# Final norm with tokens on partitions, begun inside the last products of FFN2 (decoder layer, one core)

## The chip, the cores and the metric

The kernel runs on one core of a Trainium2 chip. The time is the device time of one execution in microseconds (us), the median of three executions. The engines are named as the profile names them: PE is TensorE (PEld its weight loads), DVE is VectorE, ACT is ScalarE, POOL is GpSimd, SP is SyncE. SP issues nearly all loads and stores here.

## The reference, cut to what matters

One layer of a decoder works on 1088 tokens (1024 of a prompt, 64 of samples) of 1024 channels. Only its end matters here: the second feed-forward half step and the norm behind it.

```python
def rmsnorm(x, g):
    xf = x.astype(jnp.float32)
    y = xf * lax.rsqrt(jnp.mean(xf * xf, axis=-1, keepdims=True) + EPS)
    return (y * g.astype(jnp.float32)).astype(x.dtype)

def ffn_half_step(x, g, wg, wu, wd):
    h = rmsnorm(x, g)
    return x + 0.5 * ((jax.nn.silu(h @ wg) * (h @ wu)) @ wd)

yp = ffn_half_step(yp, ffn2_norm[l], ffn2_gate[l], ffn2_up[l], ffn2_down[l])
y_prompt = rmsnorm(yp, final_norm)
```

## The kernel before

**Layout.** The residual stream `x` lies in on-chip memory with channels on partitions: `[128, 8, 1088]`, 8 blocks of 128 channels (index d or k), the tokens along the free dimension. Token loops go over three chunks c of 384, 384 and 320 tokens. Every product is done as three passes of split operands (lines 623, 624, 625).

**Phases.** Each engine has its own instruction stream, written out by hand. Semaphores order the streams, and eleven numbered barriers (`barrier`, line 378) separate the phases: an engine drains, adds one to a shared semaphore and waits for the others. SP and POOL don't count in them; they run ahead and wait for single semaphores. Barrier 9 stands ahead of the `w_co` projection, barrier 10 ahead of the norm of FFN2, barrier 11 behind FFN2.

**FFN2.** `ffn` (PE line 635, ACT line 1135, DVE line 1523) is a loop of 11 groups of 256 hidden channels. A group first makes gate and up products into banks 0 to 3 (for each half f and chunk c, 48 matmuls). ACT takes the silu (line 1146) and rounds (1152), DVE multiplies (1542) and makes the low part (1530). Then come 24 down tiles, numbered (c, d), of 6 matmuls each, into banks 4 to 7 in turn. For each of them DVE adds half of the tile to `x` (line 1554, called the residual below). PE may write tile j only when residual j-4 is done (line 661). POOL splits the next weights (lines 569, 571) as SP's loads land; behind the last group's weights it has no work.

**Final phase.** After barrier 11, `norm` runs once more (PE 627, ACT 1119, DVE 1492) with channels on partitions. ACT squares 24 tiles of `x` (line 1126) through four buffers. PE adds them over partitions by matmuls with a matrix of ones (632), so that every partition has the token's sum. DVE scales and adds EPS (1504), ACT takes the root (1129), DVE the reciprocal of a whole 128 x 384 tile (1508) and then multiplies each of the 24 tiles of `x` by its gain and by that reciprocal, in place (1515). Only then is `x` turned: nine token tiles t of 128 tokens (the last of 64), two halves h of 512 channels, four transposes each (line 1113), into banks 0 to 3 in turn. ACT copies each half to `ytok` (1487), which has room for two token tiles, so that from t = 2 on each copy waits until the store of tile t-2 has landed (1486). SP stores each token tile, 512 KB (line 550).

```python
                act.wait_ge(F["yt"], F.base["yt"] + 2 * t + h + 1)
                if t >= 2:
                    act.wait_ge(F[f"out{t % 2}"], F.base[f"out{t % 2}"] + 16 * (t // 2))
                act.copy(ytok[0:n, t % 2, 512 * h:512 * h + 512], ps[0:n, (2 * t + h) % 4, :]).then_inc(F["tok"], 1)
```

**A phase of the same kind.** At the very start of the kernel the same statistics are taken with tokens on partitions: ACT squares a token tile and sums it along the free dimension in one instruction and the read of its accumulator (1216), DVE scales (1589), ACT takes the root of one column (1222), DVE its reciprocal (1595). The prediction takes durations from there.

Of the kernel before, what the change touches and what calls it, by code (L numbers as in the profile page):

```python
# [22 lines left out]
ALU = mybir.AluOpType  # L23
# [3 lines left out]
P = 128  # L27
D = 1024
# [14 lines left out]
EPS = 1e-6  # L43
# [56 lines left out]
def decoder_layer(nc, I, O):  # L100
# [5 lines left out]
    def alloc(stack, name, shape, dt=F32):  # L106
        return stack.enter_context(nc.sbuf_tensor(name, shape, dt))
# [15 lines left out]
    vecs = alloc(ctx, "vecs", [P, 60])  # L123
# [5 lines left out]
    early = ExitStack()  # L129
    Us = alloc(early, "Us", [P, CT, NB, PAD + TS])  # L130
    with ExitStack() as g:
        hh = alloc(g, "hh", [P, KT, T], F32R)
        hl = alloc(g, "hl", [P, KT, T], F32R)
        with ExitStack() as f:
            bh = alloc(f, "bh", [P, 2, KT, P], F32R)
            bl = alloc(f, "bl", [P, 2, KT, P], F32R)
            hidh = alloc(f, "hidh", [P, 2, T], F32R)
            hidl = alloc(f, "hidl", [P, 2, T], F32R)
            sg = alloc(f, "sg", [P, 2, 384])
            ht = alloc(f, "ht", [P, 2, 384])  # L140
            sq = alloc(f, "sq", [P, 4, 384])
            tb = alloc(f, "tb", [P, 3, 384])
            rs = alloc(f, "rs", [P, NC, 384])
        with ExitStack() as f:
# [16 lines left out]
        with ExitStack() as f:  # L161
            ytok = alloc(f, "ytok", [P, 2, D])
# [120 lines left out]
    of_tiles = {"t": NC * KT, "hi": NC * KT, "h": NC * KT}  # L283

    shared, base = {}, defaultdict(int)
    for n, adds in (("load", {"in0": 64, "in1": 64, "in2": 48, "xt": 2 * (QT + 1)}), ("n1", of_tiles | of_ffn),
                    ("nm", of_norm(NC) | of_proj(20, 12)), ("so", of_split | of_proj(8, 0)),
                    ("nx", of_norm(NC) | of_proj(8, 8)), ("sc", of_split | of_proj(8, 0)),
                    ("n2", of_norm(NC) | of_ffn), ("fin", of_norm(NC, False))):
        S[n] = Sems("g", shared, base)  # L290
        for name, v in adds.items():
            base[name] += v
    block = ctx.enter_context(nc.Block())
    x_tok = I["x_prompt"].rearrange("b t d -> (b t) d")
    xs_tok = I["x_sample"].rearrange("b t d -> (b t) d")
# [89 lines left out]
    def _(sp):  # L385
# [165 lines left out]
        sp.wait_ge(F["out0"], F.base["out0"] + 16 * ((QT + 2) // 2))  # L551
        sp.wait_ge(F["out1"], F.base["out1"] + 16 * ((QT + 1) // 2))


    @block.gpsimd
    def _(pool):
        pool.memset(ident[:], 0.0).then_inc(setup_done, 1)
        pool.memset(ones[:], 1.0).then_inc(setup_done, 1)
        pool.wait_ge(setup_done, 1)
        pool.affine_select(out=ident[:], in_=ident[:], compare_op=ALU.not_equal, fill=1.0, base=0,  # L560
                           pattern=[[-1, P]], channel_multiplier=1).then_inc(setup_done, 1)
# [55 lines left out]
    def _(pe):  # L617
        pe.sem_inc(unit_done, SLOTS)
        pe.sem_inc(row_done, 2)
        pe.wait_ge(setup_done, 3)  # L620
# [14 lines left out]
        def ffn(name, s):  # L635
            u0, c0_, r0 = UNIT[name], COL[name], ROW[name]
            with pe.Fori(0, FG) as i:
# [19 lines left out]
                for c, (c0, n) in enumerate(CHUNKS):  # L657
                    pe.wait_ge(s["hid"], s.base["hid"] + i * 6 + (NC + c + 2))
                    for d in range(KT):
                        j = c * KT + d  # L660
                        pe.wait_ge(s["res"], s.base["res"] + i * (NC * KT) + (j + 1))
                        out = ps[:, 4 + j % 4, 0:n]
                        for f in range(2):
                            mm = three(out, bh[:, f, d], bl[:, f, d], hidh[:, f, c0:c0 + n], hidl[:, f, c0:c0 + n],
                                       f == 0, f == 1)
                        if j < NC * KT - 1:
                            mm.then_inc(s["down"], 1)
                        else:
                            mm.then_inc(row_done, 2)

        def proj(name, s, nunits, chunks, ah, al, h_need):
            u0 = UNIT[name]
# [432 lines left out]
        for t in range(QT + 1):  # L1105
            n = P if t < QT else TSAMP
            pe.wait_ge(F["h"], F.base["h"] + KT * ([c for c, (c0, w) in enumerate(CHUNKS) if t * P < c0 + w][0] + 1))
            for h in range(2):
                j = 2 * t + h
                if j >= 4:  # L1110
                    pe.wait_ge(F["tok"], F.base["tok"] + j - 3)
                for k in range(4):
                    mm = pe.transpose(ps[0:n, j % 4, k * P:(k + 1) * P], x[:, 4 * h + k, t * P:t * P + n], ident[:])
                mm.then_inc(F["yt"], 1)


    @block.scalar
    def _(act):
# [15 lines left out]

        def ffn(name, s):
            c0_ = COL[name]
            with act.Fori(0, FG) as i:
                def silu(j):
                    f, c = divmod(j, NC)
                    n = CHUNKS[c][1]  # L1140
# [17 lines left out]
                hi(2 * NC - 1)  # L1158

        def store_proj(name, s, stg, nunits, first, dst):  # L1160

# [317 lines left out]
        F = S["fin"]  # L1479
        norm(F, CHUNKS, x, sq, rs, tb, hh, split=False)  # L1480
        for t in range(QT + 1):
            n = P if t < QT else TSAMP
            for h in range(2):
                act.wait_ge(F["yt"], F.base["yt"] + 2 * t + h + 1)
                if t >= 2:
                    act.wait_ge(F[f"out{t % 2}"], F.base[f"out{t % 2}"] + 16 * (t // 2))
                act.copy(ytok[0:n, t % 2, 512 * h:512 * h + 512], ps[0:n, (2 * t + h) % 4, :]).then_inc(F["tok"], 1)


    @block.vector  # L1490
    def _(dve):
# [28 lines left out]
            if split:  # L1520
                lo(KT * len(chunks) - 1)

        def ffn(name, s):
            c0_, r0_ = COL[name], ROW[name]
            with dve.Fori(0, FG) as i:
                def lo(j):
                    f, c = divmod(j, NC)
                    c0, n = CHUNKS[c]
# [18 lines left out]
                for j in range(NC * KT):  # L1547
# [4 lines left out]
                    else:  # L1552
                        dve.wait_ge(row_done, i * 2 + (2 + r0_ + 2))
                    dve.scalar_tensor_tensor(out=x[:, d, c0:c0 + n], in0=ps[:, 4 + j % 4, 0:n], scalar=0.5,  # L1554
                                             in1=x[:, d, c0:c0 + n], op0=ALU.mult, op1=ALU.add
                                             ).then_inc(s["res"], 1)

        def split_input(s):
            for c, (c0, n) in enumerate(CHUNKS):
# [74 lines left out]
        dve.tensor_copy(vecs[:], ps[:, 7, 0:60]).then_inc(L["vecs"], 1)  # L1634
# [305 lines left out]
        ffn("ffn2", S["n2"])  # L1940
        barrier(dve, 11)
        F = S["fin"]
        norm(F, CHUNKS, x, sq, rs, tb, G_FIN, hh, hl, split=False)

    ctx.close()

# [30 lines left out]
```

## Time and profile before

| | |
|---|---|
| median of 3 executions | 2907.81 us (2907.4 to 2916.08) |
| the profiled execution, own time | 2907.62 us |
| its span in the trace | 2905.8 us |
| mean granted TensorE clock | 0.963 |

Times in the trace are us from the span's start. A row of the timeline has start, length, engine, line, operation, output<-input, shapes and count; a bracket at its end tells how long the engine had been idle and what ended that. In a grouped row the numbers behind the bar are busy time and mean ns of one instruction, then the idle time ahead of them. A timeline row that merges two instructions ("x2") gives the length from the first's start to the second's end; instructions overlap, so the distance of two starts is less than the length of one.

### The profile page before, as it was taken

How to read it: one execution, taken by the hardware profiler on the slowest of the kernel's cores; microseconds unless marked ns; L12 is line 12 of the kernel's file. 1: busy time of each engine (PE TensorE's matmuls, PEld its weight loads, DVE VectorE, ACT ScalarE, POOL GpSimd, SP SyncE). 2: the span in 40 equal slices, each digit the busy share in tenths (PEclk: the TensorE clock that was granted, in tenths of full speed). 3: DMA queues.
4: the chain of work that ended last, by engine and by line, in shares of the span. 5: the costliest groups of instructions: out<-in, count | busy, mean ns of one | idle time of the engine just before them, and what ended most of it. 6: DMA issues, size and time to landing. Idle time of an engine off the chain costs nothing.

```text
span 2905.8 us, 44519 instructions
## 1 busy us (share of the span) xinstructions
PE 2666.4 (92%) x16895; PEld 2492.6 (86%) x16895; DVE 1124.5 (39%) x2110; ACT 533.8 (18%) x1178; POOL 702.9 (24%) x395
## 2 busy tenths in 40 slices
PE   6899999999998999488997988869899999999998
PEld 6899999999997999366556888739799999999997
DVE  5322222222226799633332131631523222222224
ACT  4200000000003111255221122320300000000003
POOL 4522222222220332022000210102222222222210
PEclk8999999999999999789998999989999999999999
DMA  5411111111110121144983111651111111111101
GB/s 171 145 44 43 43 43 43 43 43 43 43 43 15 44 74 63 53 154 127 287 242 108 43 46 74 229 216 44 44 44 43 43 43 43 43 43 43 43 14 62
DMA packets 214570, 223.71 MB, mean 77 GB/s; under 512 B 11466, under 2 KB 181510, under 8 KB 210403
## 3 DMA queue, kind: packets, MB, share of 16 engines
q1 hardware_dynamic: 197495, 194.54, 21.9%
q10 hardware_dynamic: 17004, 28.21, 2.6%
q8 instruction: 46, 0.75, 0.1%
q14 instruction: 25, 0.20, 0.0%
HBM read 190.05 MB, written 32.67 MB: 77 GB/s over the span
## 4 chain that ended last, share of the span: by engine, by line
PE 74%; issue 9%; DVE 7%; DMA 4%; ACT 2%; PEld 1%; DVEq 1%; SPq 1%; POOL 0%; ACTq 0%; PEldq 0%; POOLq 0%
PE ps L623 21%; PE ps L625 21%; PE ps L624 21%; DVE ya L1692 1%; PE ps L966 1%; PE ps L632 1%; PE ps L922 1%; DVE hidl L1530 1%; PE ps L849 1%; PE ps L860 1%; DMA Kw<-in_cache_win_k 1%; PE ps L936 1%; DVE hl L1497 1%; DVE rs L1508 1%; PE ps L832 1%
## 5 line engine op out<-in xcount | busy, mean ns | idle before, releaser
L623 PE MATMUL ps<-hh,wh 128*128 128x384 f32 (+1 forms) x3168 | 1039.9, 328 | 55.1 <-DVE hl L1562 29.2
L625 PE MATMUL ps<-hl,wh 128*128 128x384 f32 (+1 forms) x3168 | 1038.6, 328 | 0.0
L624 PE MATMUL ps<-hh,wl 128*128 128x384 f32 (+1 forms) x3168 | 1038.1, 328 | 0.0
L623 PEld LDWEIGHTS ps<-hh,wh 128*128 128x128 f32 x3168 | 599.5, 189 | 58.6 <-issue 57.6
L624 PEld LDWEIGHTS ps<-hh,wl 128*128 128x128 f32 x3168 | 599.6, 189 | 0.0
L625 PEld LDWEIGHTS ps<-hl,wh 128*128 128x128 f32 x3168 | 599.0, 189 | 0.0
L569 POOL CAST wh<-raw 128x1024 fp32r<-128x1024 f32 x140 | 150.9, 1078 | 1473.7 <-PE ps L625 1346.0
L1542 DVE TENSOR_TENSOR ht<-ps,sg 128x384 f32<-128x384 f32 x132 | 70.7, 536 | 927.5 <-PE ps L625 926.2
L571 POOL TENSOR_TENSOR wl<-raw,wh 128x1024 fp32r<-128x1024 f32 x148 | 378.0, 2554 | 41.7 <-ACT wh L1241 30.5
L623 PE MATMUL ps<-hidh,bh 128*128 128x384 f32 (+1 forms) x1056 | 346.5, 328 | 11.7 <-DVE x L1554 11.7
L1554 DVE SCALAR_TENSOR_TENSOR x<-ps,x 128x384 f32<-128x384 f32 (+1 forms) x528 | 276.6, 533 | 185.6 <-PE ps L625 185.1
L625 PE MATMUL ps<-hidl,bh 128*128 128x384 f32 (+1 forms) x1056 | 344.4, 326 | 0.0
L624 PE MATMUL ps<-hidh,bl 128*128 128x384 f32 (+1 forms) x1056 | 344.3, 326 | 0.0
L623 PEld LDWEIGHTS ps<-hidh,bh 128*128 128x128 f32 x1056 | 198.2, 188 | 18.4 <-DVE x L1554 18.4
L1146 ACT ACTIVATE sg<-ps 128x384 f32<-128x384 f32 x132 | 62.6, 475 | 746.5 <-PE ps L625 746.3
L624 PEld LDWEIGHTS ps<-hidh,bl 128*128 128x128 f32 x1056 | 198.2, 188 | 0.0
L625 PEld LDWEIGHTS ps<-hidl,bh 128*128 128x128 f32 x1056 | 198.2, 188 | 0.0
L1692 DVE SCALAR_TENSOR_TENSOR ya<-U,taps,ya x120 | 156.2, 1302 | 0.0
L569 POOL CAST bh<-raw 128x1024 fp32r<-128x1024 f32 x44 | 45.7, 1038 | 418.7 <-PE ps L625 417.2
L1530 DVE TENSOR_TENSOR hidl<-ht,hidh 128x384 fp32r<-128x384 f32 x132 | 133.8, 1026 | 0.1
L1146 ACT ACT_TABLE_LOAD x22 | 28.2, 1283 | 559.0 <-PE ps L625 559.0
L571 POOL TENSOR_TENSOR bl<-raw,bh 128x1024 fp32r<-128x1024 f32 x44 | 105.6, 2400 | 3.5
(215 smaller groups left out, 2168.2 us busy)
## 6 DMA issues: line engine op xcount, KB each, us to landing
raw<-in_ffn_gate SPq DMA_DIRECT2D x44, 512.0 KB, 3.8
raw<-in_ffn_up SPq DMA_DIRECT2D x44, 512.0 KB, 3.8
raw<-in_ffn_down SPq DMA_DIRECT2D x44, 512.0 KB, 3.3
Kw<-in_cache_win_k SPq DMA_DIRECT2D x48, 256.0 KB, 7.2
Vw<-in_cache_win_v SPq DMA_DIRECT2D x48, 256.0 KB
raw<-in_w_in SPq DMA_DIRECT2D x20, 512.0 KB, 3.8
Kw<-in_cache_win_k SPq DMA_DIRECT2D x8, 1024.0 KB, 11.9
Vw<-in_cache_win_v SPq DMA_DIRECT2D x8, 1024.0 KB
```

What stands on the lines that cost most here:

```text
L569: pool.tensor_copy(hi, raw[:, parity]).then_inc(w_hi, 1)
L571: pool.tensor_tensor(lo, raw[:, parity], hi.bitcast(F32), ALU.subtract).then_inc(w_split, 1)
L623: pe.matmul(out, w_hi_, a_hi, start=first, stop=False)
L624: pe.matmul(out, w_lo_, a_hi, start=False, stop=False)
L625: return pe.matmul(out, w_hi_, a_lo, start=False, stop=last)
L632: pe.matmul(ps[:, 5 + c, 0:n], ones[:], sqt[:, k % 4, 0:n], start=(k == 0), stop=(k == KT - 1)).then_inc(s["summed"], 1)
L832: mm = pe.matmul(ps[:, 2 * h + n % 2, far(t):far(t) + near(t)], qs[64 * h:64 * h + 64, p, t * P:(t + 1) * P], kTp[64 * h:64 * h + 64, p, ( ...
L1146: act.activation(sg[:, j % 2, 0:n], ps[:, 2 * (j % 2), 0:n], ACT.Silu).then_inc(s["sg"], 1)
L1530: dve.tensor_tensor(hidl[:, f, c0:c0 + n], ht[:, j % 2, 0:n], hidh[:, f, c0:c0 + n].bitcast(F32), ALU.subtract).then_inc(s["hid"], 1)
L1542: dve.tensor_tensor(ht[:, j % 2, 0:n], ps[:, 2 * (j % 2) + 1, 0:n], sg[:, j % 2, 0:n], ALU.mult).then_inc(s["prod"], 1)
L1554: dve.scalar_tensor_tensor(out=x[:, d, c0:c0 + n], in0=ps[:, 4 + j % 4, 0:n], scalar=0.5, in1=x[:, d, c0:c0 + n], op0=ALU.mult, op1=ALU.ad ...
L1692: dve.scalar_tensor_tensor(out=dst, in0=src, scalar=w, in1=dst, op0=ALU.mult, op1=ALU.add).then_inc(C["tap"], 1)
```

## The change

All parts of it stand at the end of the kernel, but for one load and a column of constants.

- The norm behind FFN2 and barrier 11 are gone. The raw `x` is turned to PSUM by PE (`turn_out`, eight transposes for a token tile, into a pair of banks that `y_bank` gives). ACT squares and sums each half out of PSUM (`y_squares`), DVE adds the two sums (`y_variance`), ACT takes the root with scale 1/1024 and EPS as its bias (`y_root`), DVE takes the reciprocal and multiplies each half by it and by the gain, from PSUM into `ytok` (`y_out`).
- `ytok` has a home for each of the nine token tiles, over the place of `hh`. No write to it waits for a store.
- The gain row is loaded broadcast to all partitions (`gain`, 512 KB written) by SP, behind the three loads of `mixx` after barrier 9. DVE waits for it ahead of FFN2.
- The loop of FFN2 runs ten times on PE, ACT and DVE, and the eleventh group is written out (on ACT for FFN1 too). In it PE turns token tile 0 behind down tile (1,3), tile 1 behind (1,7) and tile 2 behind (2,5). DVE does `y_variance` of tiles 0 and 1 behind the residuals (2,1) and (2,4), and `y_out` of them behind (2,2) and (2,5).

```diff
+        sp.dma_start(gain[:], I["final_norm"].unsqueeze(0).to_broadcast([P, D])
+                     ).then_inc(S["fin"]["small"], 16)
         col_loads("w_co", SLOTS)
         ffn_loads("ffn2")
...
-            sp.dma_start(dst, ytok[0:n, t % 2, :]).then_inc(F[f"out{t % 2}"], 16)
+            sp.dma_start(dst, ytok[0:n, t, :]).then_inc(F["out0"], 16)
...
+    def y_bank(t):
+        return (0, 2, 0, 2, 0, 2, 4, 6, 0)[t]
...
-        ffn("ffn2", S["n2"])
-        barrier(pe, 11)
-        F = S["fin"]
-        norm(F, CHUNKS, sq)
...
+        def turn_out(t):
+            n, c = P if t < QT else TSAMP, min(t // 3, NC - 1)
+            pe.wait_ge(N2["res"], N2.base["res"] + NC * KT * (FG - 1) + 4 + KT * (c + 1))
+            if t in (2, 3, 4, 5, 8):
+                pe.wait_ge(F["tok"], F.base["tok"] + 2 * ((t if t < 6 else 6) - 1))
             for h in range(2):
                 for k in range(4):
+                    mm = pe.transpose(ps[0:n, y_bank(t) + h, k * P:(k + 1) * P], x[:, 4 * h + k, t * P:t * P + n],
+                                      ident[:])
                 mm.then_inc(F["yt"], 1)
+        def beside_down(c, d):
+            for t in {(1, 3): [0], (1, 7): [1], (2, 5): [2]}.get((c, d), []):
+                turn_out(t)
+        ffn("ffn2", N2, beside_down)
+        for t in range(3, QT + 1):
+            turn_out(t)
...
-        barrier(act, 11)
-        norm(F, CHUNKS, x, sq, rs, tb, hh, split=False)
+        def y_squares(t):
+            n = P if t < QT else TSAMP
             for h in range(2):
+                j = 2 * t + h
+                act.wait_ge(F["yt"], F.base["yt"] + j + 1)
+                if t >= 4:
+                    act.wait_ge(Y["ssq"], Y.base["ssq"] + j - 7)
+                act.activation(ysq[0:n, t % 4, h, :], ps[0:n, y_bank(t) + h, :], ACT.Square,
+                               accum_out=ystat[0:n, h, t:t + 1]).then_inc(Y["ssq"], 1)
+        def y_root(t):
+            n = P if t < QT else TSAMP
+            act.wait_ge(Y["var"], Y.base["var"] + t + 1)
+            act.activation(ystat[0:n, 3, t:t + 1], ystat[0:n, 2, t:t + 1], ACT.Sqrt, bias=eps[0:n], scale=1.0 / D
+                           ).then_inc(Y["std"], 1)
+        for t in range(QT + 1):
+            y_squares(t)
+            y_root(t)
...
-        norm(F, CHUNKS, x, sq, rs, tb, G_FIN, hh, hl, split=False)
+        def y_variance(t):
+            n = P if t < QT else TSAMP
+            dve.wait_ge(Y["ssq"], Y.base["ssq"] + 2 * t + 2)
+            dve.tensor_tensor(ystat[0:n, 2, t:t + 1], ystat[0:n, 0, t:t + 1], ystat[0:n, 1, t:t + 1], ALU.add
+                              ).then_inc(Y["var"], 1)
+        def y_out(t):
+            n = P if t < QT else TSAMP
+            dve.wait_ge(Y["std"], Y.base["std"] + t + 1)
+            dve.reciprocal(ystat[0:n, 4, t:t + 1], ystat[0:n, 3, t:t + 1]).then_inc(Y["inv"], 1)
+            dve.wait_ge(Y["inv"], Y.base["inv"] + t + 1)
+            for h in range(2):
+                dve.scalar_tensor_tensor(out=ytok[0:n, t, 512 * h:512 * h + 512], in0=ps[0:n, y_bank(t) + h, :],
+                                         scalar=ystat[0:n, 4, t:t + 1], in1=gain[0:n, 512 * h:512 * h + 512],
+                                         op0=ALU.mult, op1=ALU.mult).then_inc(F["tok"], 1)
+        def beside_residual(c, d):
+            for t in {(2, 1): [0], (2, 4): [1]}.get((c, d), []):
+                y_variance(t)
+            for t in {(2, 2): [0], (2, 5): [1]}.get((c, d), []):
+                y_out(t)
+        dve.wait_ge(F["small"], F.base["small"] + 16)
+        ffn("ffn2", S["n2"], beside_residual)
+        for t in range(2, QT + 1):
+            y_variance(t)
+            y_out(t)
```

## Rows read from the trace of the kernel before

**Rows 1.** The chain that ended last, in order of time, from FFN2's last residual (start, length, what)

```profile
2865.73 0.05 DVE x L1554
...
2890.64 3.69 PE ps L1113 x16
...
2894.97 2.61 DMA out_y_prompt<-ytok
```

**Rows 2.** Instructions by line and shape, from 2866 us to the end

```profile
L1515 DVE SCALAR_TENSOR_TENSOR x<-x,vecs,rs 128x384 f32<-128x384 f32 x16 | 8.8, 607 | 0.1
L1487 ACT COPY ytok<-ps 128x512 f32<-128x512 f32 x16 | 8.7, 588 | 6.3 <-DMA out_y_prompt<-ytok 3.8 <-PE ps L1113 2.5
```

**Rows 3.** Timeline of the last down tiles and the end, DVE, ACT and SP

```profile
2854.54 0.56 DVE L1554 SCALAR_TENSOR_TENSOR x<-ps,x 128x384 f32<-128x384 f32 x1 [0.48 <-PE ps L625]
...
2858.70 0.56 DVE L1554 SCALAR_TENSOR_TENSOR x<-ps,x 128x384 f32<-128x384 f32 x1 [0.48 <-PE ps L625]
2859.57 0.49 DVE L1554 SCALAR_TENSOR_TENSOR x<-ps,x 128x320 f32<-128x320 f32 x1 [0.32 <-PE ps L625]
...
2865.73 0.49 DVE L1554 SCALAR_TENSOR_TENSOR x<-ps,x 128x320 f32<-128x320 f32 x1 [0.39 <-PE ps L625]
...
2901.44 1.06 ACT L1487 COPY ytok<-ps 64x512 f32<-64x512 f32 x2 [0.62 <-DMA out_y_prompt<-ytok]
2902.52 0.55 SPq L550 DMA_DIRECT2D out_y_sample<-ytok  x1
```

**Rows 4.** Timeline, transposes of `x` (PE) and one pair of ACT's copies

```profile
2885.86 2.03 ACT L1487 COPY ytok<-ps 128x512 f32<-128x512 f32 x4
2886.57 1.07 PE L1113 MATMUL ps<-ident,x 128*128 128x128 f32 x8 [2.31 <-DVE x L1515]
```

**Rows 5.** Timeline of the kernel's first 73 us: tokens on partitions, ACT and DVE

```profile
4.99 0.19 ACT L1216 ACTIVATION_READ_ACCUMULATOR kvtok<-xin 128x1 f32 x1
...
33.66 1.13 DVE L1621 SCALAR_TENSOR_TENSOR tb<-x,vecs,ps 128x384 f32<-128x384 f32 x2
...
66.05 0.15 DVE L1595 RECIPROCAL tstat<-tstat 128x1 f32<-128x1 f32 x1
66.24 0.29 DVE L1650 TENSOR_SCALAR diag<-ident,tstat 128x128 f32<-128x128 f32 x1
...
71.89 0.14 DVE L1589 TENSOR_SCALAR tstat<-tstat 64x1 f32<-64x1 f32 x1 [2.38 <-ACT kvtok L1216]
72.06 0.20 ACT L1222 ACTIVATE tstat<-tstat 64x1 f32<-64x1 f32 x1 [0.21 <-DVE tstat L1589]
```

**Rows 6.** All of ACT's table loads at line 1222, and DVE's copies from PSUM, whole span

```profile
L1222 ACT ACT_TABLE_LOAD  x1: 1283/1283/1283, 6.5 to 6.5; - x1
L1797 DVE COPY Kc<-ps 128x512 f32<-128x512 f32 x32 | 22.1, 691 | 47.0 <-PE ps L922 46.8
```

**Rows 7.** Stretches of time: length, busy us (count) of PE, PEld, DVE, ACT, POOL; clock, DMA share, GB/s

```profile
2886.00:2888.00 2.00, 1.07 (x8) 0.86 (x8) 2.00 (x2) 1.88 (x4) 0.00 (x0) 1.00 0.12 47
2888.00:2890.00 2.00, 0.00 (x0) 0.00 (x0) 2.00 (x5) 0.31 (x1) 0.00 (x0) 0.89 1.01 408
...
2894.00:2896.00 2.00, 2.00 (x11) 2.00 (x10) 0.29 (x1) 0.71 (x3) 0.00 (x0) 0.50 0.77 309
2896.00:2898.00 2.00, 2.00 (x17) 1.77 (x15) 0.00 (x0) 1.38 (x3) 0.00 (x0) 0.90 0.60 242
```

**Rows 8.** Around barrier 9: POOL's first split after it, and the landing of the `mixin` loads

```profile
1966.68 1.04 POOL L569 CAST wh<-raw 128x1024 fp32r<-128x1024 f32 x1 [108.98 <-PE ps L625]
...
DMA to landing us min/median/max: 6.7/10.5/13.5
```

**Rows 9.** Timeline, DVE's product (chunk 2, f=0 then f=1) in groups 0 and 10

```profile
2098.99 0.49 DVE L1542 TENSOR_TENSOR ht<-ps,sg 128x320 f32<-128x320 f32 x1 [6.03 <-PE ps L625]
...
2122.66 0.49 DVE L1542 TENSOR_TENSOR ht<-ps,sg 128x320 f32<-128x320 f32 x1 [6.01 <-PE ps L625]
...
2818.49 0.49 DVE L1542 TENSOR_TENSOR ht<-ps,sg 128x320 f32<-128x320 f32 x1 [6.01 <-PE ps L625]
...
2842.19 0.49 DVE L1542 TENSOR_TENSOR ht<-ps,sg 128x320 f32<-128x320 f32 x1 [6.01 <-PE ps L625]
```

More of the change, by code:

```diff
@@ L122, in decoder_layer @@
     ones = alloc(ctx, "ones", [P, P])
-    vecs = alloc(ctx, "vecs", [P, 60])
+    vecs = alloc(ctx, "vecs", [P, 61])
+    eps = vecs[:, 60:61]
     taps = alloc(ctx, "taps", [P, CT, CONVW])
@@ L131, in decoder_layer @@
     with ExitStack() as g:
+        with ExitStack() as f:
+            ytok = alloc(f, "ytok", [P, QT + 1, D])
+            ysq = alloc(f, "ysq", [P, 4, 2, 512])
         hh = alloc(g, "hh", [P, KT, T], F32R)
@@ L143, in decoder_layer @@
             rs = alloc(f, "rs", [P, NC, 384])
+            gain = alloc(f, "gain", [P, D])
+            ystat = alloc(f, "ystat", [P, 5, QT + 1])
         with ExitStack() as f:
@@ L160, in decoder_layer @@
             mixin = alloc(f, "mixin", [P, NC, KT, 384])
-        with ExitStack() as f:
-            ytok = alloc(f, "ytok", [P, 2, D])
         with ExitStack() as f:
@@ L285, in decoder_layer @@
     shared, base = {}, defaultdict(int)
-    for n, adds in (("load", {"in0": 64, "in1": 64, "in2": 48, "xt": 2 * (QT + 1)}), ("n1", of_tiles | of_ffn),
+    for n, adds in (("load", {"in0": 64, "in1": 64, "in2": 48, "small": 160, "xt": 2 * (QT + 1)}), ("n1", of_tiles | of_ffn),
                     ("nm", of_norm(NC) | of_proj(20, 12)), ("so", of_split | of_proj(8, 0)),
                     ("nx", of_norm(NC) | of_proj(8, 8)), ("sc", of_split | of_proj(8, 0)),
-                    ("n2", of_norm(NC) | of_ffn), ("fin", of_norm(NC, False))):
+                    ("n2", of_norm(NC) | of_ffn), ("fin", {})):
         S[n] = Sems("g", shared, base)
@@ L292, in decoder_layer @@
             base[name] += v
+    S["ys"] = Sems("st", S["st"].made, {n: MT + QT + 1 for n in ("ssq", "var", "std", "inv")})
     block = ctx.enter_context(nc.Block())
@@ L558, in _ @@
         pool.memset(ones[:], 1.0).then_inc(setup_done, 1)
+        pool.memset(eps, EPS).then_inc(setup_done, 1)
         pool.wait_ge(setup_done, 1)
@@ L619, in _ @@
         pe.sem_inc(row_done, 2)
-        pe.wait_ge(setup_done, 3)
+        pe.wait_ge(setup_done, 4)
         def three(out, w_hi_, w_lo_, a_hi, a_lo, first, last):
@@ L633, in norm, with ffn, groups @@
                               stop=(k == KT - 1)).then_inc(s["summed"], 1)
-        def ffn(name, s):
+        def ffn(name, s, beside_last=None):
             u0, c0_, r0 = UNIT[name], COL[name], ROW[name]
-            with pe.Fori(0, FG) as i:
+            def groups(i, beside=None):
                 for f in range(2):
@@ L669, in ffn @@
                             mm.then_inc(row_done, 2)
+                        if beside is not None:
+                            beside(c, d)
+            if beside_last is None:
+                with pe.Fori(0, FG) as i:
+                    groups(i)
+            else:
+                with pe.Fori(0, FG - 1) as i:
+                    groups(i)
+                groups(FG - 1, beside_last)
         def proj(name, s, nunits, chunks, ah, al, h_need):
@@ L1100, in _ @@
         norm(S["n2"], CHUNKS, sq)
-        ffn("ffn2", S["n2"])
-        barrier(pe, 11)
-        F = S["fin"]
-        norm(F, CHUNKS, sq)
-        for t in range(QT + 1):
-            n = P if t < QT else TSAMP
-            pe.wait_ge(F["h"], F.base["h"] + KT * ([c for c, (c0, w) in enumerate(CHUNKS) if t * P < c0 + w][0] + 1))
+        F, N2 = S["fin"], S["n2"]
+        def turn_out(t):
[3 more added lines that the diff above has]
+                pe.wait_ge(F["tok"], F.base["tok"] + 2 * ((t if t < 6 else 6) - 1))
             for h in range(2):
-                j = 2 * t + h
-                if j >= 4:
-                    pe.wait_ge(F["tok"], F.base["tok"] + j - 3)
                 for k in range(4):
-                    mm = pe.transpose(ps[0:n, j % 4, k * P:(k + 1) * P], x[:, 4 * h + k, t * P:t * P + n], ident[:])
+                    mm = pe.transpose(ps[0:n, y_bank(t) + h, k * P:(k + 1) * P], x[:, 4 * h + k, t * P:t * P + n],
+                                      ident[:])
                 mm.then_inc(F["yt"], 1)
+        def beside_down(c, d):
[4 more added lines that the diff above has]
+            turn_out(t)
     @block.scalar
@@ L1136, in ffn, with groups @@
             c0_ = COL[name]
-            with act.Fori(0, FG) as i:
+            def groups(i):
                 def silu(j):
@@ L1158, in ffn @@
                 hi(2 * NC - 1)
+            with act.Fori(0, FG - 1) as i:
+                groups(i)
+            groups(FG - 1)
         def store_proj(name, s, stg, nunits, first, dst):
@@ L1477, in _ @@
         ffn("ffn2", S["n2"])
-        barrier(act, 11)
-        F = S["fin"]
-        norm(F, CHUNKS, x, sq, rs, tb, hh, split=False)
-        for t in range(QT + 1):
+        F, Y = S["fin"], S["ys"]
+        def y_squares(t):
             n = P if t < QT else TSAMP
             for h in range(2):
[L1484 to L1487, printed above, removed]
+                j = 2 * t + h
[12 more added lines that the diff above has]
+            y_root(t)
     @block.vector
@@ L1521, in norm, with ffn, groups @@
                 lo(KT * len(chunks) - 1)
-        def ffn(name, s):
+        def ffn(name, s, beside_last=None):
             c0_, r0_ = COL[name], ROW[name]
-            with dve.Fori(0, FG) as i:
+            def groups(i, beside=None):
                 def lo(j):
@@ L1556, in ffn @@
                                              ).then_inc(s["res"], 1)
+                    if beside is not None:
+                        beside(c, d)
+            if beside_last is None:
+                with dve.Fori(0, FG) as i:
+                    groups(i)
+            else:
+                with dve.Fori(0, FG - 1) as i:
+                    groups(i)
+                groups(FG - 1, beside_last)
         def split_input(s):
@@ L1633, in _ @@
         dve.wait_ge(L["vecs_t"], L.base["vecs_t"] + 1)
-        dve.tensor_copy(vecs[:], ps[:, 7, 0:60]).then_inc(L["vecs"], 1)
+        dve.tensor_copy(vecs[:, 0:60], ps[:, 7, 0:60]).then_inc(L["vecs"], 1)
         dve.tensor_copy(taps[:], ps[:, 7, 64:64 + CT * CONVW].rearrange("p (k t) -> p k t", t=CONVW)
@@ L1939, in _ @@
         norm(S["n2"], CHUNKS, x, sq, rs, tb, G_FFN2, hh, hl)
-        ffn("ffn2", S["n2"])
-        barrier(dve, 11)
-        F = S["fin"]
-        norm(F, CHUNKS, x, sq, rs, tb, G_FIN, hh, hl, split=False)
+        F, Y = S["fin"], S["ys"]
+        def y_variance(t):
[22 more added lines that the diff above has]
+            y_out(t)
     ctx.close()
```

3 lines of the change are left out of this document (1 added, 2 removed).

## The prediction, before the change was run

> **What bounds the kernel now.** I read the chain of waits from its end backwards, then the instructions by line in the last 40 us, then the timeline of each engine there. The chain leaves FFN2 at 2865.73 us with the last residual; what follows is the final phase, and it takes 2905.8 - 2865.7 = 40.1 us to the end of the span [rows 1]. In it the first transpose that no longer waits for a normalised tile starts at 2890.64: some 25 us go into sums, roots, whole-tile reciprocals and the multiplications of line 1515 (16 wide ones at 0.607 us each) [rows 1, 2]. The rest goes into turning, copying and storing, where ACT waits for stores to land because `ytok` has two places: 3.8 us for full tiles [rows 2], and each such wait puts a landing of 2.61 us on the chain [rows 1]. Inside FFN2 the down tiles are PE's: DVE's residual takes 0.56 us of every 1.04, and DVE sits idle 0.48 [rows 3]. So the gain is to be found behind 2865.7, and its ceiling is 40.1 us less whatever the new end needs.
>
> **What beside the last products costs.** Three token tiles are turned inside the last group. Eight transposes take 1.07 us, 0.335 or so of it the latency of one, so they hold PE for about 0.95 us [rows 4]. PE is the bound there, so this is on the path: 3 x 0.95 = 2.85 us. ACT is idle in this stretch, its squares are covered. On DVE two `y_variance` and two `y_out` come between residuals. One `y_out` is a column reciprocal and two products of 128 x 512. Such a product is not in the trace. The nearest is the one of the same form, a column scalar and one operand in PSUM, at 384 columns: two in 1.13 us, so 0.53 from start to start and 0.60 for one [rows 5]. 64 columns more cost 0.07 us (0.49 to 0.56) [rows 3], so at 512 I take 0.67 from start to start and 0.74 for the last; from below 0.60 (the copy of 128 x 512 out of PSUM lasts 0.69) [rows 6], from above 0.9, if the two sources don't stream at that pace. With 0.19 for the reciprocal [rows 5] a `y_out` holds DVE 1.53 us. PE runs four banks ahead, 3 tiles x 0.88 us, so it does not wait.
>
> **The transition, step by step.** Product (1,3) is done at 2854.5 (its residual starts at 2854.54) and tile 0 is turned by 2855.5. Product (1,7) comes at 2859.65 instead of 2858.70, (2,0) at 2861.5 instead of 2859.57 after tile 1 is turned, (2,5) at 2865.9, the last one at 2868.6 instead of 2865.73 [rows 3]. DVE: variance 0 at 2862.8, residual (2,2), `y_out` 0 to 2865.2, two residuals, variance 1, a residual, `y_out` 1 from 2866.55 to 2868.1. Tile 2's transposes need `y_out` 0 (2865.2) and come at 2865.9: no wait. Last residual 2868.6, variance 2 at 2869.0.
>
> **The steady end, seven tiles from 2869.0.** For each tile DVE and ACT hand over twice. From the start of the variance to the start of the root 0.17 us (71.89 to 72.06), the root 0.20 and 0.03 to the reciprocal, 0.19 to the first product [rows 5], then 2 x 0.67: 1.93 us per tile if only DVE counts. The squares of the next tile run on ACT meanwhile: 0.48 from start to start (four copies of the same size in 2.03) plus 0.19 for the read of the accumulator, twice, 1.34 us [rows 4, 5]. A pair of banks gives a second loop of two tiles: end of `y_out` t, 0.04, four transposes 0.60, squares 1.34, 0.04, handshake 0.59, `y_out`'s products 1.41, that is 4.02 for two, 2.01 per tile. This one holds for tiles 4 and 5; tiles 6, 7 have banks of their own. So variance 8 starts at 2869.0 + 1.93 x 3 + 2.0 x 3 = 2880.8, and its `y_out` ends 2.0 later, at 2882.8. The stores go out one by one from 2865 and are no queue: behind the last write comes what comes today, 2905.8 - 2902.5 = 3.3 us (issue, landing, end) [rows 3]. End of the span: 2886.1.
>
> **The clock.** Today it is still at full in 2886 to 2888 with PE busy 1.07 of 2 us, falls in 2888 to 2890, in which PE is idle, and is 0.50 by 2894; at 0.5 sixteen transposes take 3.69 us, 0.23 each [rows 1, 7]. In the new end PE works about half of the time, on transposes alone. If the clock falls from 2873 on, the first half of tile 5 is ready 0.4 us later; tiles 6 to 8 are turned ahead of need at 1.85 us each. I add 0.4. The Trainium skill ("TensorE: Matmul & The Clock Gate", PE-mode transpose) says that transposes don't count as activity for the clock; by it every tile from 3 on would be turned at half clock, tiles 4 and 5 each late by 0.65 (half a tile's turning and the second half behind it), 1.3 us in place of 0.4. The row speaks against it: the clock went from 0.50 to 0.90 in 2896 to 2898 after 5 us of nothing but transposes [rows 7].
>
> **Edits with one answer.** ACT's root needs a table of its own (1.28 us), but squares after it load nothing: at the start of the kernel roots and squares alternate eleven times with one load [rows 6]. The one load here falls behind the squares of tile 0, at about 2857, with 5 us to spare. The gain load stands in SP's queue behind the three `mixin` loads (which land in 6.7 to 13.5 us) and ahead of the next `w_co` weights [rows 8]; POOL touches those first at 1966.68, when PE frees a slot, 26 us after barrier 9, and DVE wants the gain over 100 us later: nothing, and if it slows the last `mixin` chunk, at most 1 to 2 us. The written-out group: PE, DVE and ACT run fresh code once. Group 0 of FFN2 is fresh too, and its second half lasts 2122.66 - 2098.99 = 23.67 us against 23.70 in group 10 [rows 9]: nothing. The new memset and the fourth count for PE at the start lie ahead of loads that take 10 us: nothing.
>
> **Sum.** The span ends at 2886.1 + 0.4 = 2886.5 instead of 2905.8: 19.3 us less. 2907.62 - 19.3 = 2888.3 for the profiled execution; the median of the runs is 0.2 higher, so 2888.5. About 0.3% (8.7 us) is what a measurement of this kernel can tell from no change.
>
> **Rivals.**
> - *The two engines don't overlap* (chance 0.12). If DVE's reads of PSUM hold up ACT's, or ACT's in-order stream has the next squares behind a late root, each tile costs squares + handshake + products: 1.34 + 0.59 + 1.41 = 3.3 us, 7 x 1.4 = 10 more, 2898. Against it: in the sample phase ACT copies from other banks while DVE's 32 copies out of PSUM still last 0.691 on average [rows 6].
> - *Nothing is gained beside the products* (0.09): what the change says it does there is not done in effect, because DVE delays the last residuals by as much as the two tiles cost. Then two tiles of 1.93 come back: 2892.4.
> - *The stores set the end* (0.05). Nine stores of 512 KB between 2865 and 2883. At 408 GB/s, reached with two in flight [rows 7], one takes 1.3 us and fits into 1.93; if a lone stream moved only as today's 2894 to 2896 (309 GB/s, 1.7 us) it would still fit. At 150 GB/s it would be 3.5 us each: 9 x 3.5 = 31 from 2865.3, 2900 in device time.
> - *Slower: PE starves in the written-out group* (0.04). It is 432 matmuls that no loop has run before, fetched once, and all of them are on the path. Every 45 ns that one of them is late costs 19.4 us and eats the whole gain; at 65 ns the kernel is 8.7 us slower, 2916.6. The fresh group 0 speaks against it [rows 9], and so does that the other code of this size needs no second look in the chain.
> - *Half clock for every turned tile behind the products* (0.08): 1.3 in place of 0.4, 2889.4. The rule named above would give this.
> - Forecast as above: 0.62.
>
> **How the numbers follow.** The time is that of the forecast. Its own bounds: products of 0.60 instead of 0.67 give 7 x 0.14 = 1 us less, no loss to the clock 0.4, a shorter handshake 1 to 2; products of 0.9 would give 7 x 0.46 = 3.2 more, half clock throughout 0.9, the gain load 1 to 2. That makes 2885 to 2894. To leave out no more than two in ten I go up into the first rival: 2885 to 2896. Faster by over 0.3% (below 2899.1) are the forecast, half clock, nothing gained beside the products and the first rival: 0.91. Within 0.3% lies the case of the stores, 0.05; slower is the starved group, 0.04.
>
> **What the new profile would show.** DVE's variances with tokens on partitions 1.9 to 2.0 us apart; products of 128 x 512 at about 0.74; ACT's squares over before each variance; one table load for the root, ahead of the last residual; the last product of FFN2 2.9 us later than now; the last store issued near 2882.8. I am wrong if DVE idles for squares in every tile, if table loads appear between the tiles, if matmuls of the last group stand apart, or if the span's end hangs on a store older than the last.

## The result and the profile after

The kernel after the change takes 2893.28 us in the median of 7 runs (2882.7 to 2910.92), the one before 2907.81 us (2904.7 to 2923.15, 7 runs). The ratio is 0.9932, with a 95% interval of 0.9913 to 0.9951: 19.8 us faster, between 14.2 and 25.3. The medians alone differ by 14.5 us, at the edge of that interval: single runs spread too widely to say more of the whole time than that. The forecast was 2888.5 us, in a range of 2885 to 2896.

Single runs of one kernel differ by 20 us and more, much more than most of the experiments below can move. So the experiments are read by a **tail** taken inside one trace: from the start of DVE's last product of gate and up (the last `ht`, the last of [rows 9]) to the end of the span. Before it is 2905.8 - 2842.19 = 63.61 us. After it is 2883.5 - 2838.94 = 44.56 us, 19.05 less; the sum of the prediction said 19.3. The other 3.25 us by which the profiled run is shorter lie ahead of the change (last section).

Timeline of DVE after the change, last group of FFN2 to the end, cut:

```profile
2838.94 0.49 DVE L1588 TENSOR_TENSOR ht<-ps,sg 128x320 f32<-128x320 f32 x1 [6.01 <-PE ps L636]
...
2859.55 0.15 DVE L2002 TENSOR_TENSOR ystat<-ystat 128x1 f32<-128x1 f32 x1
2860.03 0.49 DVE L1600 SCALAR_TENSOR_TENSOR x<-ps,x 128x320 f32<-128x320 f32 x1 [0.32 <-PE ps L636]
2860.44 0.15 DVE L2008 RECIPROCAL ystat<-ystat 128x1 f32<-128x1 f32 x1
2860.62 1.41 DVE L2011 SCALAR_TENSOR_TENSOR ytok<-ps,ystat,gain 128x512 f32<-128x512 f32 x2
2861.95 0.88 DVE L1600 SCALAR_TENSOR_TENSOR x<-ps,x 128x320 f32<-128x320 f32 x2
...
2864.78 1.01 DVE L1600 SCALAR_TENSOR_TENSOR x<-ps,x 128x320 f32<-128x320 f32 x2
...
2866.42 1.41 DVE L2011 SCALAR_TENSOR_TENSOR ytok<-ps,ystat,gain 128x512 f32<-128x512 f32 x2
2867.75 0.15 DVE L2002 TENSOR_TENSOR ystat<-ystat 128x1 f32<-128x1 f32 x1
2868.26 0.16 DVE L2008 RECIPROCAL ystat<-ystat 128x1 f32<-128x1 f32 x1 [0.36 <-ACT ystat L1527]
2868.46 1.41 DVE L2011 SCALAR_TENSOR_TENSOR ytok<-ps,ystat,gain 128x512 f32<-128x512 f32 x2
...
2870.66 1.41 DVE L2011 SCALAR_TENSOR_TENSOR ytok<-ps,ystat,gain 128x512 f32<-128x512 f32 x2
...
2878.80 1.40 DVE L2011 SCALAR_TENSOR_TENSOR ytok<-ps,ystat,gain 64x512 f32<-64x512 f32 x2
```

Between residuals (line 1600) stand the variance, the reciprocal and the two products of tile 0, as the change says. The outputs of tiles 2, 3 and 4 start at 2866.42, 2868.46 and 2870.66: 2.04 and 2.20 us apart, the later ones 2.04 again. In each of them DVE idles 0.36 us for ACT's root. The last write ends at 2880.20.

ACT (a square and the read of its accumulator, twice, then the table and the root of tile 0) and SP:

```profile
2851.89 0.60 ACT L1521 ACTIVATE ysq<-ps 128x512 f32<-128x512 f32 x1 [11.96 <-PE ps L1133]
2852.38 0.19 ACT L1521 ACTIVATION_READ_ACCUMULATOR ysq<-ps 128x1 f32 x1
2852.47 0.59 ACT L1521 ACTIVATE ysq<-ps 128x512 f32<-128x512 f32 x1
2852.95 0.20 ACT L1521 ACTIVATION_READ_ACCUMULATOR ysq<-ps 128x1 f32 x1
2853.17 1.28 ACT L1527 ACT_TABLE_LOAD   x1
2859.74 0.29 ACT L1527 ACTIVATE ystat<-ystat,vecs 128x1 f32<-128x1 f32 x1 [5.29 <-DVE ystat L2002]
...
2880.22 0.55 SPq L561 DMA_DIRECT2D out_y_sample<-ytok  x1
```

The table is loaded once and 5.29 us ahead of need. The first row and the third start 0.58 us apart: that is what a square and its read cost ACT, as the read overlaps both neighbours. The last store is issued 3.3 us before the end of the span, as before [rows 3].

Stretches of the same end (columns as in [rows 7]):

```profile
2866.00:2868.00 2.00, 0.16 (x3) 0.05 (x1) 1.64 (x4) 1.41 (x6) 0.00 (x0) 1.00 0.50 203
2868.00:2870.00 2.00, 1.04 (x8) 0.82 (x9) 1.63 (x4) 1.49 (x5) 0.00 (x0) 1.00 0.65 262
2870.00:2872.00 2.00, 1.98 (x18) 2.00 (x19) 1.60 (x5) 1.56 (x5) 0.00 (x0) 1.00 0.65 262
2872.00:2874.00 2.00, 1.70 (x16) 1.43 (x14) 1.60 (x5) 1.45 (x5) 0.00 (x0) 1.00 0.55 225
...
2876.00:2880.00 4.00, 0.00 (x0) 0.00 (x0) 3.21 (x9) 1.73 (x6) 0.00 (x0) 0.84 0.63 258
```

PE's transposes behind the last product:

```profile
2867.98 1.06 PE L1133 MATMUL ps<-ident,x 128*128 128x128 f32 x8 [1.84 <-DVE ytok L2011]
2870.02 3.69 PE L1133 MATMUL ps<-ident,x 128*128 128x128 f32 x32 [0.97 <-DVE ytok L2011]
```

DVE is busy 1.6 of 2 us. PE is full in 2870 to 2872 only because it turns tiles 5 to 8 in one go, ahead of need, and it is done at 2873.7; ACT has pauses throughout. So DVE with its hand-over to ACT sets the end. The clock is at full as long as PE has anything to do, and the stores take 0.65 of the DMA engines.

### The profile page after: what moved, and what is told of

Same layout as the page of the kernel before. It is cut to its first block, busy times and chain, and to the rows that moved or that the text cites. A ratio compares the mean times of both kernels' runs of the same rounds, so it can differ in the third digit from the quotient of the medians.

```text
span 2883.5 us, 44318 instructions
## 1 busy us (share of the span) xinstructions
PE 2645.7 (92%) x16847; PEld 2478.5 (86%) x16847; DVE 1118.2 (39%) x2116; ACT 522.6 (18%) x1176; POOL 703.0 (24%) x396
## 4 chain that ended last, share of the span: by engine, by line
PE 74%; issue 9%; DVE 8%; DMA 4%; ACT 2%; PEld 1%; DVEq 1%; SPq 1%; POOL 0%; ACTq 0%; PEldq 0%; POOLq 0%
PE ps L634 21%; PE ps L636 21%; PE ps L635 21%; DVE ya L1748 1%; PE ps L988 1%; PE ps L944 1%; DVE hidl L1576 1%; PE ps L871 1%; PE ps L882 1%; PE ps L958 1%; DVE hl L1542 1%; DMA Kw<-in_cache_win_k 1%; PE ps L854 1%; PE ps L1038 1%; PE ps L643 1%
```

## The experiments

**Homes alone.** The old final phase, with nine places in `ytok` and no wait for stores.

```diff
-                if t >= 2:
-                    act.wait_ge(F[f"out{t % 2}"], F.base[f"out{t % 2}"] + 16 * (t // 2))
-                act.copy(ytok[0:n, t % 2, 512 * h:512 * h + 512], ...
+                act.copy(ytok[0:n, t, 512 * h:512 * h + 512], ...
```

> The old final phase with one edit: a home for each of the nine output tiles, so no copy waits for a store. The measure in all these runs is the tail: from the start of DVE's last product of gate and up (the last ht) to the end of the span; before 63.6 us, with the change 44.6. Theory (the homes were a small part): the transposes behind the last multiplied tile run without a pause and the last copy is some 2.6 us earlier, tail 61. Rival (the stores on the chain were the main cost, 2.61 us for each landing there): tail 55 to 58.

Tail 2906.6 - 2845.44 = 61.16 us, 2.45 less. The waits for stores are gone, and what is late next is the turning (PE, ACT, and a stretch with columns as in [rows 7]):

```profile
2893.89 7.96 PE L1112 MATMUL ps<-ident,x 128*128 128x128 f32 x48 [3.01 <-DVE x L1512]
2895.04 0.59 ACT L1484 COPY ytok<-ps 128x512 f32<-128x512 f32 x1 [2.94 <-PE ps L1112]
2895.89 0.59 ACT L1484 COPY ytok<-ps 128x512 f32<-128x512 f32 x1 [0.27 <-PE ps L1112]
```

```profile
2894.00:2896.00 2.00, 2.00 (x10) 2.00 (x11) 2.00 (x5) 0.69 (x2) 0.00 (x0) 0.50 0.45 180
```

PE turns 48 blocks without a pause. Behind its idle time of 3.01 us the granted clock is 0.50 up to 2898, and as long as it is, ACT waits 0.27 us for each half; the last seven copies follow each other without a wait. Two landings of 2.61 us stood on the chain before, yet taking both away gave 2.45 in all.

**Two places in the new form.** The reverse: the change, with `ytok` of two places and the wait put back, on DVE.

```diff
+            if t >= 2:
+                dve.wait_ge(F[f"out{t % 2}"], F.base[f"out{t % 2}"] + 16 * (t // 2))
             for h in range(2):
-                dve.scalar_tensor_tensor(out=ytok[0:n, t, ...
+                dve.scalar_tensor_tensor(out=ytok[0:n, t % 2, ...
```

> The change, but with ytok of two places again, so that the output of tile t waits for the store of tile t-2. Theory: a store lands 2.6 us after its issue and the output of tile t starts 2.67 us after that of t-2 ended, so the wait is nearly covered: tail 44.6 to 46.5, I take 45.3; homes are worth next to nothing in the new form. Rival (homes matter as they did before, a landing on the chain for every second tile): tail 50 or more.

Tail 2897.5 - 2852.51 = 44.99 us, 0.43 more than the change. One wait is open, ahead of tile 7:

```profile
2890.72 1.41 DVE L2014 SCALAR_TENSOR_TENSOR ytok<-ps,ystat,gain 128x512 f32<-128x512 f32 x2 [0.35 <-DMA out_y_prompt<-ytok]
```

So the homes are worth 2.45 us in the old order and 0.43 in the new one: an output every 2.04 us leaves a store time to land.

**Nothing beside the products.** All nine tiles behind the last residual, FFN2 a loop of eleven groups.

```diff
-        ffn("ffn2", N2, beside_down)
-        for t in range(3, QT + 1):
+        ffn("ffn2", N2)
+        for t in range(QT + 1):
             turn_out(t)
```

(and the same on DVE and ACT)

> The new norm, but all nine tiles behind the last residual, and FFN2 a loop of eleven groups again. Theory: 2.85 us of transposes leave FFN2 and two more tiles of 2.04 to 2.1 us plus the first tile's turning and squares (about 2) come behind it; tail 48, so work beside the products is worth 3.4 us. Rival (nothing gained beside, DVE delays the last residuals by as much): tail 44.6 to 45.

Tail 2894.9 - 2845.03 = 49.87 us. The new norm alone, with its homes, gives 13.74 of the 19.05 us, the work beside the products 5.31, more than the 3.4 us that were expected. The outputs of tiles 2, 3, 4, 5 and 6 start 2.21, 2.76, 2.21, 2.77 and 2.03 us after the one ahead. Timeline and stretches show two causes:

```profile
2870.29 1.28 ACT L1525 ACT_TABLE_LOAD   x1
2870.30 0.16 DVE L2000 TENSOR_TENSOR ystat<-ystat 128x1 f32<-128x1 f32 x1 [1.24 <-ACT ysq L1519]
2871.58 0.29 ACT L1525 ACTIVATE ystat<-ystat,vecs 128x1 f32<-128x1 f32 x1
...
2873.66 1.06 PE L1133 MATMUL ps<-ident,x 128*128 128x128 f32 x8 [3.39 <-DVE ytok L2009]
...
2875.70 1.94 PE L1133 MATMUL ps<-ident,x 128*128 128x128 f32 x8 [0.97 <-DVE ytok L2009]
```

```profile
2874.00:2876.00 2.00, 1.03 (x9) 0.82 (x8) 1.67 (x4) 1.45 (x5) 0.00 (x0) 0.65 0.65 262
2876.00:2878.00 2.00, 1.73 (x9) 1.36 (x8) 1.57 (x3) 1.13 (x4) 0.00 (x0) 0.50 0.65 262
```

The load of the root's table now stands on the path, and behind a pause of 3.39 us of PE the clock falls to 0.50: eight transposes take 1.94 us in place of 1.06. The next two runs take these apart.

**PE kept busy.** The same, and PE turns blocks that nobody reads in its pauses (added work).

```diff
+            if t < 5:
+                idle_turns((8, 28, 8, 8, 8)[t])
```

> As with nothing beside, but PE fills its pauses behind tiles 0 to 4 with 8, 28, 8, 8 and 8 turns of a block into a bank that nobody reads (added work, the output is unchanged). In the run with nothing beside, the outputs of tiles 3 and 5 came 2.76 us after the one ahead while the granted clock was 0.50 (tail 49.87). Theory (PE's pause of 3.4 us ahead of tile 2 let the clock fall, and slow turning costs the two tiles 0.7 us each): the clock stays at 1.00, all intervals 2.0 to 2.2, tail 48.4. Rival (turned blocks don't count as activity, or the 2.76 come from the banks): clock 0.50 and the same intervals, tail 49.9 or more.

Tail 2899.3 - 2850.52 = 48.78 us, 1.09 less, though the added turns themselves made tile 2 later by 0.35 (2.56 in place of 2.21). The intervals of tiles 3 and 5 are 2.03 and 2.04. The clock:

```profile
2876.00:2878.00 2.00, 2.00 (x20) 2.00 (x19) 0.56 (x2) 1.99 (x5) 0.00 (x0) 1.00 0.00 0
2878.00:2880.00 2.00, 2.00 (x21) 2.00 (x20) 1.60 (x5) 0.82 (x3) 0.00 (x0) 1.00 0.08 31
2880.00:2882.00 2.00, 2.00 (x21) 2.00 (x20) 1.21 (x4) 1.59 (x6) 0.00 (x0) 1.00 0.64 258
```

It is 1.00 through stretches in which PE does nothing but transposes, and with it the 2.76 us are gone. The rival falls.

**The root's table early.** Nothing beside, and one root on ACT ahead of the first squares.

```diff
+        act.activation(ystat[:, 4, QT:QT + 1], eps, ACT.Sqrt)
         for t in range(QT + 1):
             y_squares(t)
```

> As with nothing beside, plus one root of a column on ACT right behind its last work of FFN2, so that the root's table is loaded before the first squares. Theory (with nothing beside, the load of 1.28 us stands open ahead of the first root): the first output starts 1.1 us earlier, and PE's pause is as much shorter; tail 48.8, or 47.4 if the shorter pause also keeps the clock up. Rival (the squares load a table of their own again): tail 49.9 to 51.

Tail 2889.3 - 2841.34 = 47.96 us, 1.91 less. The first output starts 25.99 instead of 27.08 us behind the last `ht`, 1.09 earlier, as expected; PE's pause is 2.30 us, the clock falls all the same (0.50 in 2872 to 2874 of that trace) but comes back sooner: the intervals of tiles 3 to 5 are 2.63, 2.14 and 2.10 us in place of 2.76, 2.21 and 2.77, and that is the rest of the 1.91. Both cures together were not tried. The added root has neither a column as bias nor a scale, and it is shorter than the 0.29 us of the roots with both:

```profile
2843.64 0.20 ACT L1528 ACTIVATE ystat<-vecs 128x1 f32<-128x1 f32 x1
```

**Only PE and ACT beside.** Tiles 0 and 1 turned beside the products, DVE's part of them behind. Tile 2 is turned behind the last residual too (on PE, not shown):

```diff
         def beside_residual(c, d):
-            for t in {(2, 1): [0], (2, 4): [1]}.get((c, d), []):
-                y_variance(t)
-            for t in {(2, 2): [0], (2, 5): [1]}.get((c, d), []):
-                y_out(t)
+            return
```

> The change, but only PE and ACT work beside the products (tiles 0 and 1 turned and squared there); all of DVE's statistics and outputs come behind the last residual, and tile 2 is turned there. Theory (DVE sets the end, so only its work taken ahead pays): nine tiles of 2.04 us behind the last residual, tail 47.7, hardly better than with nothing beside (48). Rival (the transposes and squares taken ahead are what pays): tail 45.5.

Tail 2908.2 - 2858.85 = 49.35 us: higher than expected, since two intervals of 2.77 stand in this run too, but only 0.52 under nothing beside. ACT's part was taken ahead only for tile 0. Its instructions run in their order, and the squares of tile 1 stand behind the root of tile 0, which waits for DVE:

```profile
2884.90 0.29 ACT L1527 ACTIVATE ystat<-ystat,vecs 128x1 f32<-128x1 f32 x1 [10.55 <-DVE ystat L2002]
2885.11 0.58 ACT L1521 ACTIVATE ysq<-ps 128x512 f32<-128x512 f32 x1
```

No variance waits for these late squares, so they cost nothing. Of the 4.79 us that this run lies above the change, about 1.5 are the slow turning (2.77 in place of 2.04, twice, behind a pause of PE of 2.71 us); the rest is DVE's two outputs, less the tile that PE no longer turns inside FFN2. So it is DVE's work taken ahead that pays, as the theory has it.

**Squares behind the output.** The change with one more wait on ACT.

```diff
+                if t >= 3:
+                    act.wait_ge(F["tok"], F.base["tok"] + 2 * t)
```

> The change, with an added wait on ACT: from tile 3 on its squares start only when the output of the tile ahead is done, which is the serial course that the first rival of the prediction feared. Theory (ACT's squares run beside DVE's output for nothing in the change): each of six tiles costs 1.24 more for the squares, 3.3 us from output to output, tail 44.6 + 7.7 = 52.3. Rival (the two are already serial in effect): tail 44.6 to 45.5.

Tail 2898.3 - 2844.91 = 53.39 us, the outputs 3.54 us apart from tile 3 on. Against 2.04 and one 2.20 that is 8.8 us more, where 7.7 were expected: beside the 1.26 us of squares the new wait brings its own passing to and fro. This is the price of the first rival of the prediction, and the change does not pay it.

**Variance ahead.** Four pairs of banks, and the sums of tile t+1 are added ahead of the output of tile t.

```diff
+            if t < QT:
+                y_variance(t + 1)
             y_out(t)
```

> The change with four pairs of banks behind the last residual and DVE adding the sums of tile t+1 ahead of the output of tile t, so that the hand-over to ACT's root and back (0.5 us per tile) is covered. Theory (the cycle of 2.04 us is hand-over 0.7 and two products of 0.67): from tile 4 on the outputs come 1.7 us apart, bound by ACT, tile 3 comes 0.7 us later since its root waits for the squares of tile 4; tail 43.3. Rival (the cycle is set by something else, PE or the banks): intervals stay 2.04, tail 45.

Tail 2891.3 - 2848.53 = 42.77 us, 1.79 less than the change. DVE, timeline:

```profile
2880.07 1.41 DVE L2015 SCALAR_TENSOR_TENSOR ytok<-ps,ystat,gain 128x512 f32<-128x512 f32 x2
2881.47 0.16 DVE L2006 TENSOR_TENSOR ystat<-ystat 128x1 f32<-128x1 f32 x1
2881.55 0.15 DVE L2012 RECIPROCAL ystat<-ystat 128x1 f32<-128x1 f32 x1
2881.74 1.41 DVE L2015 SCALAR_TENSOR_TENSOR ytok<-ps,ystat,gain 128x512 f32<-128x512 f32 x2
```

Variance and reciprocal stand 0.08 us apart, with no wait for the root between them; outputs from tile 5 to tile 7 come 1.67 us apart. So waiting for the root cost 0.37 of the 2.04 us. More was not to be had in this form, because the next limit is close: ACT's root and the squares behind it take 1.67 us from one variance to the next, and DVE's own work takes 1.59, the interval of tile 4.

**The written-out group alone.** Nothing beside, but the eleventh group written out.

> Nothing beside the products, but the eleventh group written out as in the change. Theory (fresh code costs nothing): the last group is as long as in the loop, last residual 24.03 us behind the last ht, tail 49.9 as in the loop. Rival (the prediction's slower case, PE waits for its code): the last group's 24 down tiles or its 288 gate and up matmuls take longer, 19 us and more for the case to matter.

Tail 2898.6 - 2848.55 = 50.05 us, the last residual ends 24.19 us behind the last `ht` against 24.03: 0.16 us. (The tail begins only behind the gate and up matmuls; from the last residual of group 9, at 2801.16, to the last `ht` are 47.39 us, against 47.56 from 2794.63 to 2842.19 before.) Fresh code costs nothing that matters.

**Six tiles beside, and a shorter hand-over.** Tiles 0 to 5 turned and 0 to 4 put out between the residuals; then the same with the sums of tiles 7 and 8 added between the two halves of the output ahead.

```diff
-            for t in {(1, 3): [0], (1, 7): [1], (2, 5): [2]}.get((c, d), []):
+            for t in {(1, 0): [0], (1, 2): [1], (1, 4): [2], (2, 1): [3], (2, 3): [4], (2, 6): [5]}.get((c, d), []):
                 turn_out(t)
```

> The change with tiles 0 to 5 turned behind (1,0), (1,2), (1,4), (2,1), (2,3), (2,6) and DVE's outputs of tiles 0 to 4 between the residuals. Theory: FFN2's end moves from 26.85 to about 29.7 to 31 us behind the last ht (six turned tiles of 0.95 and DVE nearly full), and only four outputs of 2.04 us stand behind it; tail 42.5. Rival (DVE becomes the bound of the down tiles and gives back what the tail saves): tail 44 to 46.

> The same with DVE adding the sums of tiles 7 and 8 between the two halves of the output ahead, so that ACT's root runs beside the second half. Theory: two intervals of 2.04 become about 1.85; tail 42.1, time of the whole 21 to 22 us under the kernel before, with the spread of single runs far larger than the 2.5 us under the change. Rival (the squares of the next tile are not done by the middle of the output): no shorter than with six tiles alone.

Tails 2900.2 - 2858.25 = 41.95 us and 2889.9 - 2848.48 = 41.42 us. The last residual ends 30.4 us behind the last `ht`, 3.5 later than in the change, and only four outputs follow it. The second is the shortest tail of all runs: 3.14 us less than the change. Its time is 2890.48 us in the median of 6 runs (2880.74 to 2895.43), ratio 0.9919 to the kernel before (0.9896 to 0.9942). That interval holds the change's 0.9932 too; that it beats the change rests on the tails. Nothing was tried that joins it with the variance ahead.

## Why the prediction was right

In order of its steps, times counted from the last `ht`:

- **Transposes beside the products.** Said 2.85 us on the path; the last residual ends 26.85 instead of 24.03 behind the last `ht`, 2.82.
- **An output on DVE.** Said 0.67 and 0.74 for the products that no row showed, 1.53 us in all. Measured 1.41 for the pair, which is 0.67 + 0.74, and 1.51 from reciprocal to the next residual.
- **The transition.** The last residual was to start 26.4 behind the last `ht` (2868.6 - 2842.19) and does so at 26.36; PE's matmuls follow each other without a gap, so it never waits for a bank.
- **The cycle: too short.** Said 1.93 us, and 2.01 where the banks count. Measured 2.04, and 2.20 for tile 4. The root takes 0.29 us, not the 0.20 of line 1222 [rows 5], which had neither a column as bias nor a scale (the added root above, without either, takes 0.20 too; which of the two costs the time was not tested). PE starts 0.14 us after the output it waits for, not 0.04. ACT's squares were set too high, 1.34 against 1.26 with the last read, which is off the path in all tiles but tile 4. That tile is the only one that the banks hold up; the sum had counted three intervals of 2.0. Over seven tiles the last write came at 41.3, not 40.6.
- **The clock: a loss that did not come.** The 0.4 us for it were wrong. The prediction let the clock fall from 2873 on, which is 30.8 us behind the last `ht` in the trace before. After the change PE turns its last tile up to 34.8 us behind it, and until then the clock is at full. The fall of [rows 7], from which the prediction argued, came in a stretch in which PE was idle: in the middle of a pause of 3.01 us, which followed one of 2.31 us [rows 4]. The longest pause in the change is 1.84 us. Where it was 2.30, 2.71 and 3.39 us (the runs with the table early, with DVE's outputs late and with nothing beside) the clock did fall to 0.50 and cost up to 0.7 us in each of two tiles. So the loss is real where PE waits long for the first outputs; the change avoids it since its first outputs come beside the products. The prediction did not work that out. The Trainium skill ("TensorE: Matmul & The Clock Gate", PE-mode transpose) would have had tiles turned at half clock from tile 3 on, 1.3 us in place of 0.4. Both traces differ: 1.00 from 2866 to 2874 with nothing but transposes, and again with PE kept busy.
- **Sum.** 19.3 us said, 19.05 measured: the two errors, 0.65 more and 0.4 less, nearly cancel, and that is luck. The median of 2893.3 lies 4.8 over the forecast and the profiled run 3.0 under it. For the profiled run the trace shows where that comes from: 3.25 us lie ahead of the last `ht`. The median run has no trace. Only three of the seven runs lie between 2885 and 2896, since the range left out the spread of single runs; that the median fell into it owes something to luck too. What the record bears out is the tail.
- **Edits costed at nothing.** One table load, covered. The written-out group 0.16 us. The gain load was covered: from the first load of `mixin` after barrier 9 to the last `ht` it is 901.2 us after the change and 902.0 before. See below for what it does to SP's queue.
- **The rivals.** Engines that don't overlap: priced at 10 us more, made to happen it was 8.8, and in the change it does not. Nothing gained beside the products: priced at 3.9, and 5.3 when the work was left out there altogether, since the table load and the clock come on top; it did not happen. Stores that set the end: they take 0.65 of the DMA engines and one wait of 0.35 us opens when they are given just two places. PE starved: no.

## What to carry to other kernels

Work at the end of a kernel is worth its own path and not its busy time: here 24 wide multiplications, whole-tile reciprocals and partition sums gave way to nine short chains, and what bounds them is one engine's output plus a hand-over of column-sized steps. Take ahead the work of the engine that will set the end (5.3 us with DVE's outputs beside the products, 0.5 with PE's and ACT's part alone; some 1.5 of the difference is the clock), and look what else the early start covers: a table load, the clock. A wait for a store may stand on the chain and still be worth less than it shows, since the next thing is nearly as late (5.2 us on the chain, 2.45 when gone, 0.43 in the new order).

## What was not expected of the hardware

**Most of the spread of the runs has one place.** In the thirteen traces of this study the last `ht` starts between 2838.9 and 2858.9 us, and what lies ahead of it is almost the same code in all of them. Most of it arises in the sample attention, which streams the window caches: from DVE's first copy of keys to the load of `mixin` it lasts 161.3 us in the trace after the change and 183.6 in the one with DVE's outputs late, the shortest and the longest. The time ahead of this stretch spreads by 9.1 us and the time from it to the last `ht` by 6.1. That stretch (columns as in [rows 7]) after the change, then its larger key loads (KB each, us from issue to landing), then the same two views of the other run:

```profile
1386.80:1548.10 161.30, 147.03 (x984) 81.20 (x984) 58.34 (x185) 39.54 (x79) 0.00 (x0) 0.98 0.86 243
```

```profile
Kw<-in_cache_win_k SPq DMA_DIRECT2D x7, 1024.0 KB, 11.9
```

```profile
1381.50:1565.10 183.60, 150.50 (x985) 82.29 (x984) 58.35 (x185) 39.55 (x79) 0.00 (x0) 0.93 0.84 214
```

```profile
Kw<-in_cache_win_k SPq DMA_DIRECT2D x7, 1024.0 KB, 19.1
```

DVE and ACT are busy for the same time; the loads move at 214 instead of 243 GB/s and land in 19.1 instead of 11.9 us. Why they do was not looked into, so it stays open. A gain of a few us at the end of this kernel can be seen in a trace, and in medians only over many runs.

**Behind the `mixin` loads SP's queue is slow, whatever comes next.** SP's issues after barrier 9, after the change, then the first weight load to be held up there:

```profile
1937.74 3.10 SPq L436 DMA_DIRECT2D mixin<-mixx_scratch  x3
1940.88 3.95 SPq L550 DMA_DIRECT2D gain<-in_final_norm  x1
1944.94 34.31 SPq L397 DMA_DIRECT2D raw<-in_w_co  x4
```

```profile
1945.40 4.30 SPq L397 DMA_DIRECT2D raw<-in_w_co  x1
```

The issue of the gain row to 128 partitions takes 3.95 us, a store of the same 512 KB at the kernel's end 0.33. It looks as if the broadcast were to blame. The trace before the change, which has no gain load, says otherwise:

```profile
1940.19 3.19 SPq L427 DMA_DIRECT2D mixin<-mixx_scratch  x3
1943.49 3.86 SPq L388 DMA_DIRECT2D raw<-in_w_co  x1
```

There a plain weight load of 512 KB stands behind the three `mixin` loads, and its issue takes 3.86 us. So the place costs the time and not the form of the load; whether the broadcast adds anything of its own was not tested. The weights are issued about 4 us later than before, counted from the first `mixin` load, and nothing comes of it: POOL takes up the first of them at 1963.48, when PE frees a slot, 18.5 us after their issue begins. `mixin` lands in 6.5 to 13.3 us, against 6.7 to 13.5 before [rows 8].
